# A two-layer hybrid decoder step on one core: queries projected before all keys, side products' copies placed after the chain beside them, tables made later

## What is computed

```
h = rmsnorm(x, g_attn)
(q_a, kv_cmp, kv_slc, kv_win, gate_a, q_b, k_b, v_b, r_b, lr_b, merge) = split(h @ w_in)
q = rmsnorm(q_a, g_q) * Dh ** -0.5                    # per head of 64
kv_slc, kv_win: keys rmsnorm'ed per head; kv_cmp is kept raw
kv_c = compress_kv(cmp_all, w_cmp1, w_cmp2)           # blocks of 32 rows, stride 16
o_a = gates * (cmp_attend, sel_attend, win_attend)    # compressed, selected, window
o_b = gated linear attention (q_b, k_b, v_b, lr_b, r_b)
x += (sigmoid(gA) * (o_a @ w_pa) + sigmoid(gB) * (o_b @ w_pb)) @ w_out
x += (gelu(causal_dwconv3(h2 @ w_u)) * (h2 @ w_g)) @ w_down
```

## Time and profile before

| | us |
|---|---|
| median of 3 runs | 2773.48 (2773.33 to 2778.31) |
| profiled execution, its own time | 2782.36 |
| its span, first to last instruction | 2780.5 |
| TensorE busy | 2510.3 (90%) |
| VectorE busy | 804.2 (29%) |
| ScalarE busy | 525.9 (19%) |
| GpSimd busy | 97.4 (4%) |
| mean granted TensorE clock | 0.935 of full |

### The profile page before, as it was taken

One profiled execution on the slowest core, in us unless ns is written; L12 is line 12 of the kernel. 1 busy time (PEld: TensorE's weight loads), 2 busy tenths in 40 slices (PEclk: granted clock), 3 DMA queues, 4 the chain that ended last, 5 costly groups with the idle time before them and its releaser, 6 DMA issues.

```text
span 2780.5 us, 31038 instructions
## 1 busy us (share of the span) xinstructions
PE 2510.3 (90%) x13198; PEld 2013.2 (72%) x13198; DVE 804.2 (29%) x1827; ACT 525.9 (19%) x1053; POOL 97.4 (4%) x182
## 2 busy tenths in 40 slices
PE   6887788997898999999998877789888989999998
PEld 5676556676787888888876755666677878888886
DVE  2344332545312121210015443225433122121001
ACT  1253110442100111110013421014511011111100
POOL 3010000000000000000000100000000000000000
PEclk8997889997999999999999978889979999999999
DMA  7244411100121122212262524211111212221231
GB/s 231 71 153 174 167 61 52 40 19 30 46 79 61 61 76 67 70 54 79 69 200 87 199 95 167 76 46 31 31 33 55 69 50 72 76 76 62 54 83 64
DMA packets 184576, 228.52 MB, mean 82 GB/s; under 512 B 37470, under 2 KB 170932, under 8 KB 180084
## 3 DMA queue, kind: packets, MB, share of 16 engines
q1 hardware_dynamic: 174008, 133.11, 16.1%
q0 software_dynamic: 10432, 93.44, 8.7%
HBM read 218.19 MB, written 16.66 MB: 84 GB/s over the span
## 4 chain that ended last, share of the span: by engine, by line
PE 83%; DVE 8%; ACT 5%; DMA 2%; issue 2%; DVEq 0%; SPq 0%; ACTq 0%; POOLq 0%
PE PS L783 47%; PE PS L1314 12%; PE PS L805 5%; ACT arena L1345 4%; PE PS L899 4%; PE PS L887 2%; DVE arena L1598 2%; PE PS L1127 2%; PE PS L1138 2%; PE PS L426 2%; DVE arena L1607 1%; DMA arena<-in_state_kv_win_dram 1%; PE PS L1008 1%; PE PS L1236 1%; DMA arena<-in_cache_kv_slc_dram,idx 1%
## 5 line engine op out<-in xcount | busy, mean ns | idle before, releaser
L783 PE MATMUL PS<-hT,ring 128*128 128x272 f32 x4608 | 1089.0, 399 | 10.6 <-DVE hT L1604 10.6
L783 PEld LDWEIGHTS PS<-hT,ring 128*128 128x128 f32 x4608 | 888.0, 193 | 204.9 <-issue 19.5
L1345 ACT ACTIVATE arena<-PS 64x512 f32<-64x512 f32 (+9 forms) x496 | 245.1, 517 | 1428.3 <-PE PS L783 722.2
L1314 PE MATMUL PS<-arena,ring 128*128 128x272 f32 x1408 | 323.5, 393 | 1.9 <-DVEq L2156 1.9
L1314 PEld LDWEIGHTS PS<-arena,ring 128*128 128x128 f32 x1408 | 267.2, 190 | 57.6 <-DVEq L2156 2.7
L1607 DVE COPY arena<-PS 64x512 f32<-64x512 f32 (+7 forms) x215 | 155.7, 725 | 334.4 <-PE PS L783 141.5
L1598 DVE TENSOR_TENSOR arena<-PS,arena 128x544 f32<-128x544 f32 (+3 forms) x120 | 73.0, 621 | 502.2 <-PE PS L783 425.0
L783 PE MATMUL PS<-arena,ring 128*128 128x272 f32 x768 | 177.2, 393 | 3.2 <-DVE arena L1598 3.2
L1604 DVE SCALAR_TENSOR_TENSOR arena<-arena,prm 128x32 f32<-128x32 f32 (+2 forms) x178 | 90.5, 509 | 292.4 <-ACT arena L1345 289.2
L783 PEld LDWEIGHTS PS<-arena,ring 128*128 128x128 f32 x768 | 145.8, 190 | 33.9 <-DVE arena L1598 4.0
L899 PE MATMUL PS<-arena 128*128 128x256 f32 (+1 forms) x576 | 140.3, 389 | 24.3 <-DVE arena L1598 19.6
(11 more groups left out here) (271 smaller groups left out, 1654.4 us busy)
## 6 DMA issues: line engine op xcount, KB each, us to landing
ring<-in_w_up_dram SPq DMA_DIRECT2D x88, 512.0 KB, 4.2
ring<-in_w_in_dram SPq DMA_DIRECT2D x68, 512.0 KB, 4.7
ring<-in_w_down_dram SPq DMA_DIRECT2D x32, 384.0 KB, 3.8
ring<-in_w_down_dram SPq DMA_DIRECT2D x32, 320.0 KB, 4.5
arena<-in_state_kv_win_dram POOLq DMA_DIRECT2D x4, 2048.0 KB, 8.4
ring<-in_w_out_dram SPq DMA_DIRECT2D x16, 512.0 KB, 4.1
out_dram<-in_state_kv_win_dram POOLq DMA_DIRECT2D x2, 4064.0 KB, 22.4
ring<-in_w_in_dram SPq DMA_DIRECT2D x16, 256.0 KB, 4.5
```

The source lines that it names most:

```text
L783: mm = pe.matmul(PS[0:m, b + a, 0:HALF], weight(k), rhs(k)[:, HALF * a:HALF * a + HALF], start=(k == 0), stop=(k == nk - 1))
L1314: mm = pe.matmul(PS[:, b + a, 0:HALF], w[:, k, :], aT[:, 11 * half + k, HALF * a:HALF * a + HALF], start=(half == 0 and k == 0), stop=(hal ...
L1345: return nc.scalar.activation(out, in_, func, **kw)
```

## The change

It has three parts. (1) The layer's first projections go in the order q0 to q3, kv1, kv2, kv0. The slab of q2 and q3 becomes the second one loaded; the loads of kv2 and kv0 are issued behind the wait for `layer_done`, `w_cmp` and `gup`. All four query norms follow kv1; `few` goes ahead of `tm`; the fold is two tickets, `kvf` for the two key branches and `kvf0` for the compressed one; the keys' norm (`keys_ready`) no longer waits for the compressed values, and `kv_ready`, for which the stores wait, is signalled later. (2) VectorE's tables are made in the first layer behind `n1`'s normalization; TensorE waits for `consts` only before the first query norm, and GpSimd makes `fold4`, `fold2`, `gup` and part of `lrT` after `consts`, with a signal `fold_consts` of their own. (3) `side_copy(("c", qt, 0))` stands behind the last product of the softmax chain, `pc_p`.

```diff
-    steps = ["q0", "kv1", "kv2", "kv0", "q1", "gl", "qb", "kb", "rb0", "rb1", "vb0", "vb1"]
+    steps = ["q0", "q1", "kv1", "kv2", "kv0", "gl", "qb", "kb", "rb0", "rb1", "vb0", "vb1"]
...
                 query_cols(0)
+                query_cols(1)
                 cols_of("kv1", w_in, O_KV + 256)
-                cols_of("kv2", w_in, O_KV + 512)
 
                 sp.wait_ge(*S.at(sp, "layer_done", 0))
...
+                cols_of("kv2", w_in, O_KV + 512)
                 cols_of("kv0", w_in, O_KV)
-                query_cols(1)
...
             gp.nop().then_inc(*S.inc(gp, "consts"))
+            for v in (fold4[:, :], fold2[:, :], gup[:, :], lrT[:, P:NT]):
+                gp.memset(v, 0.0).then_inc(*S.inc(gp, "pool_step"))
+                gp.wait_ge(*S.last(gp, "pool_step"))
...
+            gp.nop().then_inc(*S.inc(gp, "fold_consts"))
...
-            pe.wait_ge(*S.at(pe, "consts", 1))
...
-                for r in range(2):
-                    fm("T", f"q{r}", wload("q0"), P * r, ready=None if r else ("h_ready", 0))
-                for j in (1, 2, 0):
-                    s = wload(f"kv{j}")
-                    tm(f"kv{j}a", s, 0, 256, 256, range(4))
-                    few(f"kv{j}b", s, 256)
-                for r in range(2):
+                for r in range(R):
+                    fm("T", f"q{r}", wload(f"q{r // 2}"), P * (r % 2), ready=None if r else ("h_ready", 0))
+                s = wload("kv1")
+                few("kv1b", s, 256)
+                tm("kv1a", s, 0, 256, 256, range(4))
+                pe.wait_ge(*S.at(pe, "consts", 0))
+                for r in range(R):
                     pe.wait_ge(*S.at(pe, "sq_q", r + 1))
                     product("S", f"qn{r}", lambda k: mean_h[:, :], lambda k: sq_q[:, r, :], 1)
-                fm("T", "q2", wload("q1"), 0)
+                s = wload("kv2")
+                few("kv2b", s, 256)
+                tm("kv2a", s, 0, 256, 256, range(4))
+                pe.wait_ge(*S.at(pe, "fold_consts", 0))
                 pe.wait_ge(*S.claim(pe, "T", "kvf"))
...
+                pe.matmul(PS[0:NS, b, :], fold4[:, :], kvs[:, 1:3, :].rearrange("p j n -> p (j n)"), start=True, stop=True).then_inc(*S.fill(pe, "kvf"))
+                s = wload("kv0")
+                few("kv0b", s, 256)
+                tm("kv0a", s, 0, 256, 256, range(4))
...
+                pe.matmul(PS[0:NS, b, 0:256], fold4[:, :], kvs[:, 0, :], start=True, stop=True).then_inc(*S.fill(pe, "kvf0"))
                 s = wload("gl")
...
-                for r in range(2, R):
-                    pe.wait_ge(*S.at(pe, "sq_q", r + 1))
-                    product("S", f"qn{r}", lambda k: mean_h[:, :], lambda k: sq_q[:, r, :], 1)
...
-                pe.wait_ge(*S.at(pe, "kv_ready", 1))
+                pe.wait_ge(*S.at(pe, "keys_ready", 1))
...
+                def value_key(j):
+                    act.wait_ge(*S.filled(act, f"kv{j}b"))
+                    b = S.banks(act, f"kv{j}b")
+                    run(kvs[:, j, :], PS[:, b, 0:256], ACT.Copy).then_inc(*S.drain(act, f"kv{j}b"))
                     act.wait_ge(*S.filled(act, f"kv{j}a"))
                     b = S.banks(act, f"kv{j}a")
                     run(kv[:, 0:4, j, :], PS[:, b:b + 2, :].rearrange("p a (t n) -> p (a t) n", t=2), ACT.Copy).then_inc(*S.drain(act, f"kv{j}a"))
...
+                for r in range(R):
+                    query(r)
+                value_key(1)
+                for r in range(R):
+                    query_root(r)
+                value_key(2)
...
                 run(skv, skv, ACT.Sqrt, bias=eps_c, scale=1.0 / HD).then_inc(*S.inc(act, "k_root"))
-                query(3)
+                value_key(0)
+                act.wait_ge(*S.filled(act, "kvf0"))
...
                 normed("n1", PR_ATTN)
+                dv.wait_ge(*S.at(dv, "consts", 0))
+                tsc(qcol, qscale, gm(PR_GQ), ALU.mult).then_inc(*S.inc(dv, "qcol"))
+                if l == 0:
+                    S.phase(dv, "pro")
+                    tables()
+                    S.phase(dv, "loop", l)
...
-                query_scale(0)
-                query_scale(1)
-                for j in range(3):
+                for r in range(R):
+                    query_scale(r)
+                for j in (1, 2):
                     dv.wait_ge(*S.drained(dv, f"kv{j}a"))
...
-                last.then_inc(*S.inc(dv, "kv_ready"))
-                query_scale(2)
-                query_scale(3)
+                last.then_inc(*S.inc(dv, "keys_ready"))
...
+                dv.wait_ge(*S.at(dv, "keys_ready", 1))
+                dv.wait_ge(*S.drained(dv, "kv0a"))
+                dv.wait_ge(*S.drained(dv, "kvf0"))
+                dv.nop().then_inc(*S.inc(dv, "kv_ready"))
...
                     tt(zp[:, :, :], zp[:, :, :], bc(slope_row[:, :].unsqueeze(2), [P, HEADS, NBLK_P]), ALU.mult).then_inc(*S.inc(dv, "zp"))
-                    side_copy(("c", qt, 0))
                     dv.wait_ge(*S.at(dv, "ecp", qt + 1))
...
                     tt(zpm[:, :, :], zpm[:, :, :], bc(small[:, 88:96].unsqueeze(2), [P, HEADS, NBLK_P]), ALU.mult).then_inc(*S.inc(dv, "pc_p"))
+                    side_copy(("c", qt, 0))
                     if qt < QT - 1:
```

More of the change, by code:

```diff
@@ L218, in last_ticket @@
     if name[:2] == "kv":
-        return name + "b"
+        return name + "a"
     if name[:2] in ("pa", "pb"):
@@ L589, in _ @@
             gp.nop().then_inc(*S.inc(gp, "first_consts"))
-            for v in (fold4[:, :], fold2[:, :], gup[:, :], lrT[:, P:NT], group_sum[:, :], mean_h[:, :], spread[0:NS, :, :], kv[:, 4, :, :], gates[:, 4, :], qbd[:, :, :]):
+            for v in (group_sum[:, :], mean_h[:, :], spread[0:NS, :, :], kv[:, 4, :, :], gates[:, 4, :], qbd[:, :, :]):
                 gp.memset(v, 0.0).then_inc(*S.inc(gp, "pool_step"))
@@ L625, in _ @@
             gp.wait_ge(*S.last(gp, "pool_step"))
[L626 to L631, removed]
             for r in range(R):
@@ L657, in _ @@
             gp.nop().then_inc(*S.inc(gp, "consts"))
+            for v in (fold4[:, :], fold2[:, :], gup[:, :], lrT[:, P:NT]):
+                gp.memset(v, 0.0).then_inc(*S.inc(gp, "pool_step"))
+                gp.wait_ge(*S.last(gp, "pool_step"))
+            for q in range(4):
+                select(fold4[:, :], [[-1, NS]], -NS * q, 1, ALU.not_equal, 1.0).then_inc(*S.inc(gp, "pool_step"))
+                gp.wait_ge(*S.last(gp, "pool_step"))
+            for q in range(2):
+                select(fold2[:, :], [[-1, 24]], -GL_HALF * q, 1, ALU.not_equal, 1.0).then_inc(*S.inc(gp, "pool_step"))
+                gp.wait_ge(*S.last(gp, "pool_step"))
+            gp.nop().then_inc(*S.inc(gp, "fold_consts"))
             gp.wait_ge(*S.at(gp, "tables", 1))
@@ L1673, in normed, with tables @@
                         stt(hT[:, k, :], xT[:, k, :], gm(g0 + k), rst[:, :], ALU.mult, ALU.mult).then_inc(*S.inc(dv, "h_ready"))
-                normed("n1", PR_ATTN)
+                def tables():
+                    dv.wait_ge(*S.at(dv, "consts", 1))
+                    rsum(head_of[:, :], ident[:, :].rearrange("p (b h t) -> p h b t", b=4, t=TS), mybir.AxisListType.XY)
+                    rsum(small[:, 64:68], ident[:, :].rearrange("p (a t) -> p t a", t=TS))
+                    rsum(small[:, 72:80], ident[:, :].rearrange("p (a e) -> p e a", e=8)).then_inc(*S.inc(dv, "table_step"))
+                    dv.wait_ge(*S.last(dv, "table_step"))
+                    tt(small[:, 80:88], head_of[:, :], slope_row[:, :], ALU.mult)
+                    tt(small[:, 88:92], small[:, 64:68], t_row[:, 0:4], ALU.mult)
+                    rsum(g0_c, head_of[:, 0:4])
+                    rsum(g1_c, head_of[:, 4:8])
+                    tt(small[:, 96:104], small[:, 72:80], t_row[:, :], ALU.mult).then_inc(*S.inc(dv, "table_step"))
+                    dv.wait_ge(*S.last(dv, "table_step"))
+                    rsum(slope_c, small[:, 80:88])
+                    rsum(t_c, small[:, 88:92])
+                    rsum(h8_c, small[:, 96:104]).then_inc(*S.inc(dv, "table_step"))
+                    dv.wait_ge(*S.last(dv, "table_step"))
+                    tsc(nslope_c, slope_c, -1.0, ALU.mult)
+                    tsc(dslc[:, :], dslc[:, :], t_c, ALU.subtract)
+                    tsc(dcmp_s[:, :], dcmp_s[:, :], t_c, ALU.subtract)
+                    tsc(dwin[:, :], dwin[:, :], t_c, ALU.subtract)
+                    tsc(dnew[:, :, :], dnew[:, :, :], t_c, ALU.subtract).then_inc(*S.inc(dv, "table_step"))
+                    dv.wait_ge(*S.last(dv, "table_step"))
+                    table_tmp = carve(8192, 576)
+                    tsc(table_tmp[:, 0:512], dwin[:, :], float(-WIN), ALU.is_le, NEG, ALU.mult)
+                    tsc(table_tmp[:, 512:576], dnew[:, :, :].rearrange("p a n -> p (a n)"), 0.0, ALU.is_gt, NEG, ALU.mult).then_inc(*S.inc(dv, "table_step"))
+                    dv.wait_ge(*S.last(dv, "table_step"))
+                    tt(dwin[:, :], dwin[:, :], table_tmp[:, 0:512], ALU.add)
```

(5 more changed lines are left out.)

58 lines of the change are left out of this document (7 added, 51 removed).

## The result

The changed kernel takes 2734.34 us (median of 4 runs, 2728.49 to 2740.43) where the kernel before, run beside it, takes 2775.38 us (4 runs, 2773.33 to 2778.31). The ratio is 0.9852, its 95% interval 0.9827 to 0.9876: 41 us less, with the interval from 34 to 48. The forecast was 2729, range 2717 to 2744.

A forecast was written before the change was run, and what follows sets the result against it. The prediction took TensorE's matmuls as the bound (83% of the chain), with gains only from its idle time and lower clock. Terms summed to 44.2 us: 2782.4 profiled became 2738.2, less 8.9 for the median 2729.3; range 2717 to 2744.

The forecast's parts named there:

- Part 3, waits: Prompt's compressed attention: TensorE's 20.8 us of waits at the transposes go but for 0.3 per layer, 20.2 us gained.
- The rival in which the moved copies become waits of several us: TensorE's next side product waits for the bank pair VectorE copies late; about 7 us come back, 2736; chance 0.06.
- Part 3, clock: Prompt's compressed attention: slow stretches behind the removed pauses mostly return to full clock, 6 of 9.3 us, from 0 to 9.3.
- Part 1, waits: Projections, first query to first turn: 7.7 us of waits go, 2.9 come back; 4.8 us per layer, 9.6 in all.
- The give-backs: Projections: new short TensorE waits for bank-pair copies, at gate (1.5 us) and at the first turn, 2.9 us per layer.
- the sum: All gains added: 4.7 + 9.6 + 3.7 + 20.2 + 6.0 = 44.2 us.
- The clock at the first turn: First turn and product behind it: without the 7.00 us pause, 0.9 and 2.8 us of slow clock return, 3.7 together.
- Part 2: Start: n1 no longer waits for GpSimd's consts and begins near 20.1 us; 4.7 us gained, bounds 3.5 and 6.4.
- a shorter slow start: Start: a shorter pause before n1 leaves less slow clock, so 4.7 us are gained where the lower bound is 3.5.
- The loads: Second layer's q2 slab lands at 1421 to 1423, costing 0 to 2 us, taken as nothing; kv1 and kv2 hidden.
- a rival at 5 us: Second layer: q2's slab lands late, TensorE stands up to 4 us and restarts at low clock, 2734; chance 0.08.
- The slower rival: Both layers: kv2's load comes late on SyncE's queue and TensorE waits, price 50 us, 2779; chance 0.02.

The follow-up runs named there:

- side_only: The kernel before with only the side copies moved behind the last product of the softmax chain: 2746.54 us, ratio 0.9891.
- warm_pauses: The kernel before with TensorE's pauses ahead of the pct turns and the first turn filled with throwaway identity products, no wait removed: 2757.16 us, ratio 0.9932.
- proj_only: The kernel before with only the new order of the projections and their loads, tables and side copies as before: 2768.68 us, ratio 0.9970.
- tables_only: The kernel before with only the tables made later and the wait for the constants moved: 2771.85 us, ratio 0.9986.
- slab_late: The changed kernel with the load of q2's and q3's slab put behind layer_done, w_cmp and gup: 2764.75 us, ratio to before 0.9962.

## Why the prediction was right, point by point

**Part 3, waits: right.** Taken 20.2, measured 19.7. The new wait at the few-row product was seen and priced at 0.3 us per layer; it is 0.54. It stands where the forecast put it, behind a copy of 1.24 us. The rival in which the moved copies become waits of several us is refuted: no other wait of that kind exists in the changed kernel.

**Part 3, clock: right.** The term was 6.0 of a counted 9.3 us. In the pair of profiles the two stages shortened by 27.8 us, which less 19.7 of waits is 8.1; in side_only it is 9.7; over all profiles it is 6.8. So the term has the right size, and these data can't tell 6.0 from 9.3. warm_pauses shows the cause directly: TensorE busy in the pauses, without a wait removed, wins back clock in the work behind them.

**Part 1, waits: right.** Taken 4.8 per layer, measured 5.2 and 3.6 in the change, 5.4 and 3.6 in proj_only. The give-backs of the first layer came as listed, 2.87 against 2.9 us. The idle time fell from 8.10 to 2.87 us; the sum had counted 7.7 of the 8.10 and left out two bank waits of 0.20 us that went too. VectorE and ScalarE were late nowhere else. The second layer's missing 1.2 us are slower products, at the first queries and at the keys' transposes.

**The clock at the first turn: right at its rows, not shown in the time.** 3.7 us were taken. In the change the turn went from 3.31 to 1.94 and from 3.65 to 2.52 us, the second layer's first product behind it from 3.75 to 1.97, 4.3 us in all. This repeats: in the three kernels with an idle pause there (before, side_only, tables_only) the turn took 3.27 to 3.65 us and the product 3.75 in four of six cases; in the four without fillers in which the pause is gone the turn took 1.94 to 3.40 and the product 1.96 or 1.97 in all eight. On average that is 2.2 us per layer, 4.4 in all. warm_pauses, with the pause filled, has 1.94 twice. But the time of proj_only is 7.3 us less, with 11.7 as its bound, where waits and clock together would make over 13. Which of the two is off stays open. Profiled executions differ from their medians: that of before took 2782.36 us, above all eighteen runs of before that go with proj_only, and its second compressed stage, 267.3 us, is the longest in the table. Of the 7.7 us by which that stage fell in the change, only the rows at the turn, 2.9 us, are shown to be the change's. The recorded text also says that the second layer's compressed stage was 1.9 us longer than the first's; cut at the places of the table it was 5.1 us longer.

**Part 2: right in kind, a term too large.** Taken 4.7, measured 3.5 in the pair, the lower bound, and 2.9 as the average over the four old and four new starts without a filler. The removed wait moved `n1` by 3.4 us as worked out; the 1.2 us for a shorter slow start didn't come, and this is the term that was mis-sized. The clock had fallen to 0.91 in the window 18 to 19 and to 0.50 by 19, and was slow for 5.5 us of the product as before. The Trainium skill, "TensorE: Matmul & The Clock Gate", section "Part 1: The HAM clock gate", says that the same kernel meets a different number of slow matmuls from run to run. The profiles agree: in the four that keep the old start, `n1` began between 23.52 and 23.58 us and the same 32 records took 9.38, 9.56, 9.77 and 10.42 us. The tables and the later gathers cost nothing, as argued.

**The loads: hidden, with 3 us to spare.** The price of a load issued just behind the gathers was read correctly from before (25.6 us now, 26.9 then). The sum had it landing 0 to 2 us late and took nothing for it, with a rival at 5 us; 3 us of slack decided. kv2 was not near being late: in the first layer it was issued from 69.73 and wanted at 86.3 us, in the second its issue stands first in the row at 1405.39. The slower rival had nothing to stand on. It would have needed a load that is wanted first and issued last: slab_late built one, and lost 30 us of waits.

**The sum.** 44.2 us forecast between profiled executions, 48.1 found. Of these 40.1 lie in the stages that were changed: 3.5 + 8.8 + 27.8, against 4.7 + 9.6 + 26.2 = 40.5 forecast for them. The rest, 8.0 us against 3.7, lies in stages without a change; what of it belongs to the change, beyond the rows at the first turn, isn't shown. The medians show 41.0 us, 3.2 less than forecast. The other 1.9 us between 2729.3 and 2734.3 are the starting point: the forecast took 2773.5 for the kernel before, and its median beside the change is 2775.38. That single terms came out above and below and nearly cancelled is in part luck; the two large terms, the waits of part 3 and part 1, did not need it.

## What to carry to other kernels

Where matmuls set the pace, a short wait can cost twice: its idle time, and the slow clock behind it (here 19.7 us of waits took 7 to 10 us of clock with them). Look for VectorE waiting on a side product while it holds a softmax chain that TensorE needs next; whatever is ready goes first, and the copy that has a free bank pair goes last. Price a removed wait by its idle time, and the clock behind it from the same rows in several profiles, not from one; and if a pause can't be removed, fill it with throwaway products in a bank that is claimed anyway. Before moving a load next to gathers, work out when it is issued and read from the trace what a load issued just behind them took: here 25.6 and 26.9 us.

## What the runs showed of the hardware that I had not expected

- Throwaway products in pauses, with every wait kept, took 18.8 us off a kernel of 2776 and 14.7 us off one of 2734.
- A slow stretch need not lie beside an idle pause, and a busy TensorE can stay slow for long. At 490 to 500 us before and at 469.5 to 479.5 us in the change it is busy 10.00 of 10.00 us at 0.51 and 0.50, and at 670 to 680 us in the change again at 0.50. The first of these places is slow in eighteen of twenty cases, whether the pauses of the stage before it are idle, filled or gone. I can't say what brings it on.
- 256 KB in rows of 256 bytes, issued 0.5 us after the first of the gathers, took 25.6 us to land; the same kind of load takes 4.9 us by the page's median. While the gathers ran, SyncE's own issues stood for 17.64 us.
- The same instructions of the compressed stage took between 258.0 and 267.3 us in seven profiles, of two layers each. A term of under 4 us that is read from one execution's clock can't be found again in the length of such a stage. It can be found in the rows just behind the pause, when several profiles are laid side by side. In the time, 4 to 11 runs of a kernel left intervals of 5 to 10 us.
